# Two transformer blocks on one core: x and the meta tokens laid out turned by the host, small vectors in one block

## What is computed

```python
meta = broadcast(meta_tokens)                      # 16 tokens
x = concatenate([meta, x], axis=1)                 # 272 x 1024
h = rms_norm(x, attn_norm_g)                       # x * rsqrt(mean(x*x) + 1e-6) * g
proj = einsum('bld,de->ble', h, w_in)
qa, ka, va, qb, kb, vb = split(proj, splits)       # 512, 128, 128, 512, 512, 512 columns
qb = apply_rope(rms_norm(qb by heads of 64, b_q_norm_g), ang_b)      # the same for kb, qa, ka
lam = exp(sum(b_lambda_q1 * b_lambda_k1)) - exp(sum(b_lambda_q2 * b_lambda_k2)) + 0.2
```

## Time and profile before

| | |
|---|---|
| median of 3 runs | 814.72 us (813.7 to 815.52) |
| profiled execution, its own time | 815.82 us |
| its span, first to last instruction | 814.3 us |
| mean granted TensorE clock | 0.971 |
| busy: TensorE, VectorE, ScalarE, GpSimd | 96%, 57%, 46%, 14% |
| moved by DMA | 128.68 MB, 158 GB/s over the span |

### The profile page before, as it was taken

How to read it: one execution, slowest core, us unless ns; L and a number is a source line. 1 busy time by engine, 2 the same in 40 slices (tenths; PEclk the granted TensorE clock), 3 DMA queues, 4 the chain that set the end, 5 groups by cost and what they waited for, 6 DMA issues and landing times.

```text
span 814.3 us, 11050 instructions
## 1 busy us (share of the span) xinstructions
PE 779.4 (96%) x4468; PEld 676.4 (83%) x4468; DVE 465.1 (57%) x651; ACT 372.8 (46%) x539; POOL 110.4 (14%) x133
## 2 busy tenths in 40 slices
PE   5989897999999999999999999999988999999996
PEld 4777687789999999988888888887867998888995
DVE  3888734456555555555756666475586664444432
ACT  4454555245444444435543525383445554444431
POOL 3678305020000000003000000000020111111110
PEclk9999876999999999999999999999999999999999
DMA  9534204187666556633653545245372675555521
GB/s 222 181 97 132 79 1 130 36 271 227 215 190 188 183 171 193 182 101 119 204 195 114 198 150 192 70 131 198 136 232 81 217 245 184 184 183 185 188 64 52
DMA packets 70610, 128.68 MB, mean 158 GB/s; under 512 B 5264, under 2 KB 29056, under 8 KB 70560
## 3 DMA queue, kind: packets, MB, share of 16 engines
q1 hardware_dynamic: 68512, 123.75, 47.6%
q0 software_dynamic: 1808, 4.08, 2.1%
q10 hardware_dynamic: 240, 0.15, 0.1%
HBM read 126.85 MB, written 1.05 MB: 157 GB/s over the span
## 4 chain that ended last, share of the span: by engine, by line
PE 87%; DVE 5%; POOL 3%; ACT 2%; DMA 2%; issue 1%; SPq 0%; ACTq 0%; DVEq 0%; POOLq 0%
PE psum L372 45%; PE psum L653 27%; PE psum L419 3%; PE psum L515 2%; PE psum L583 2%; PE psum L672 2%; DMA w_raw<-in_w_in 2%; PE psum L773 1%; PE psum L434 1%; PE psum L559 1%; PE psum L713 1%; PE psum L443 1%; PE psum L397 1%; POOL head_square_sums L1662 1%; POOL vb_meta L1718 1%
## 5 line engine op out<-in xcount | busy, mean ns | idle before, releaser
L1156 DVE TENSOR_TENSOR w_lo<-w_raw,w_hi 128x1024 fp32r<-128x1024 f32 x224 | 272.2, 1239 | 159.9 <-ACT w_hi L820 158.8
L820 ACT ACTIVATE w_hi<-w_raw 128x1024 fp32r<-128x1024 f32 x232 | 238.1, 1061 | 154.7 <-PE psum L653 85.9
L653 PE MATMUL psum<-h_hi,w_hi 128*128 128x256 f32 x608 | 171.8, 283 | 1.3 <-DVE h_lo L1169 0.8
L653 PE MATMUL psum<-h_lo,w_hi 128*128 128x256 f32 x608 | 171.9, 283 | 0.0
L653 PE MATMUL psum<-h_hi,w_lo 128*128 128x256 f32 x608 | 171.2, 282 | 0.0
L372 PE MATMUL psum<-w_hi,h_hi 128*128 128x512 f32 (+1 forms) x352 | 141.7, 402 | 7.9 <-DVE w_lo L1156 4.6
L372 PE MATMUL psum<-w_hi,h_lo 128*128 128x512 f32 (+1 forms) x352 | 138.9, 395 | 0.0
L372 PE MATMUL psum<-w_lo,h_hi 128*128 128x512 f32 (+1 forms) x352 | 138.8, 394 | 0.0
L653 PEld LDWEIGHTS psum<-h_hi,w_hi 128*128 128x128 f32 x608 | 114.7, 189 | 2.6 <-issue 1.9
L653 PEld LDWEIGHTS psum<-h_hi,w_lo 128*128 128x128 f32 x608 | 114.9, 189 | 0.0
L653 PEld LDWEIGHTS psum<-h_lo,w_hi 128*128 128x128 f32 x608 | 114.3, 188 | 0.6
(11 more groups left out here) (301 smaller groups left out, 983.6 us busy)
## 6 DMA issues: line engine op xcount, KB each, us to landing
w_raw<-in_w_in SPq DMA_DIRECT2D x78, 512.0 KB, 4.6
w_raw<-in_w_down SPq DMA_DIRECT2D x54, 512.0 KB, 4.2
w_raw<-in_w_up SPq DMA_DIRECT2D x32, 512.0 KB, 4.6
w_raw<-in_w_gate SPq DMA_DIRECT2D x44, 256.0 KB, 2.9
w_raw<-in_w_up SPq DMA_DIRECT2D x44, 256.0 KB, 3.2
w_raw<-in_w_out SPq DMA_DIRECT2D x16, 512.0 KB, 4.4
w_raw<-in_w_branch_a SPq DMA_DIRECT2D x4, 512.0 KB, 5.1
w_raw<-in_w_branch_b SPq DMA_DIRECT2D x4, 512.0 KB, 5.2
```

The source lines that it names most:

```text
L653: mm = pe.matmul(outs, x[:, cols], y[:, kc, :], start=kc == 0 and n == 0, stop=kc == KC - 1 and n == 2)
L820: act.activation(T.w_hi[:, k % SLOTS, :], T.w_raw[:, k % RAW_SLOTS, :], ACT.Copy).then_inc(S.w_rounded, 1)
L1156: dve.tensor_tensor(T.w_lo[:, k % SLOTS, :], T.w_raw[:, k % RAW_SLOTS, :], T.w_hi[:, k % SLOTS, :], ALU.subtract).then_inc(S.w_cut, 1)
```

## The change

The host writes x and the meta tokens, transposed, into one array (turned, 128 x 8 x 272), the gains transposed, the rope table with the eight broadcast vectors as 4 KB rows for each partition (vectors, 0.5 MB), and ident with subln (small). On the chip:

- SyncE's queue has a quarter of turned ahead of each of the fills 0 to 3. Small, vectors and x itself come behind fill 5. GpSimd issues no early DMA.
- ScalarE's queue has gains, meta tokens and the meta rope rows.
- TensorE's transposes of gains, x and meta tokens are gone; its first instruction is the first product of slab "qb".
- ScalarE and VectorE take h_hi and h_lo straight from turned, which lies in the space of the later attention maps, chunk by chunk; fill 0 is rounded and cut in two halves, and the first product waits for the first half alone.
- The squares of x stand on ScalarE behind the rounding of fill 5, the mean on VectorE behind cut 5 and the lambda products; the meta tokens are scaled behind the last h_lo.

```diff
--- before.py
+++ after.py
...
+def laid_out(inputs):
+    arrays = {name: np.ascontiguousarray(inputs[name]) for name in _INS}
+    rope, arrays["rope2"] = rope_tables()
+    arrays["mask"] = masks()
+    tokens = np.concatenate([inputs["x"][0], inputs["meta_tokens"]], axis=0)
+    arrays["turned"] = np.ascontiguousarray(tokens.T.reshape(KC, P, KEYS).transpose(1, 0, 2))
+    gains = [inputs[name][0] for name in ("attn_norm_g", "ffn_norm_g", "norm_mix_pre_2", "norm_mlp_pre_2")]
+    arrays["gains"] = np.ascontiguousarray(np.stack(gains).reshape(4, KC, P).transpose(2, 0, 1))
+    arrays["small"] = np.ascontiguousarray(np.concatenate([np.eye(P, dtype=np.float32), inputs["b_subln_g"].T], axis=1))
+    rows = [rope[:SEQ].reshape(TILES, P, 4 * HD).transpose(1, 0, 2).reshape(P, TILES * 4 * HD)]
+    for name in ("a_q_norm_g", "a_k_norm_g", "b_q_norm_g", "b_k_norm_g", "b_lambda_q1", "b_lambda_k1", "b_lambda_q2",
+                 "b_lambda_k2"):
+        rows.append(np.broadcast_to(inputs[name], (P, HD)))
+    arrays["vectors"] = np.ascontiguousarray(np.concatenate(rows, axis=1))
+    arrays["rope1m"] = np.ascontiguousarray(rope[SEQ:])
+    return arrays
...
+    T.xt = T.maps[:, 0]
...
 def sync_program(nc, a, out, T, S, W):
     sp = nc.sync
-    for t in range(TILES):
-        sp.dma_start(T.x[:, t, :], a["x"][0, t * P:(t + 1) * P, :]).then_inc(S.x_landed[t], 16)
     for k, pieces in enumerate(W.fills):
         r = k % RAW_SLOTS
+        if k < KC // 2:
+            sp.dma_start(T.xt[:, 2 * k:2 * k + 2, :], a["turned"][:, 2 * k:2 * k + 2, :]).then_inc(S.turned_landed[k], 16)
+        if k == RAW_SLOTS + 2:
+            sp.dma_start(T.small[:], a["small"]).then_inc(S.small_landed, 16)
+            sp.dma_start(T.vectors[:], a["vectors"]).then_inc(S.small_landed, 16)
+            for t in range(TILES):
+                sp.dma_start(T.x[:, t, :], a["x"][0, t * P:(t + 1) * P, :]).then_inc(S.x_landed[t], 16)
...
@@ TensorE, slab @@
-            pe.wait_ge(*W.cut(S, k))
+            if not first or j > 0:
+                pe.wait_ge(*W.cut(S, k))
             for c in range(per):
                 kc = j * per + c
+                if first:
+                    pe.wait_ge(S.first_cut, kc + 1)
+                if first and j == 0:
+                    pe.wait_ge(*((S.half_cut, 1) if c == 0 else W.cut(S, k)))
...
-    pe.wait_ge(S.ident_landed, 16)
-    pe.wait_ge(S.gain_landed, 16)
-    pe.transpose(bank[7][:, 0:KC], T.gain_rows[0:KC, :], ident[0:KC, 0:KC]).then_inc(S.gains_turned, 1)
-    x_ready = [[(S.x_landed[t], 16)] for t in range(TILES)]
-    turn_pairs(T.x, (0,), (3,), x_ready)
-    turn_pairs(T.x, (1,), (4,), [(), ()])
-    turn_pairs(T.x, (2, 3), (5, 6), [(), ()])
-
-    def gains_and_meta():
...
-    slab("qb", KC, ((0,), (1,)), ready=CUT["h1"], between={(1, 1): gains_and_meta})
+    slab("qb", KC, ((0,), (1,)), first=True)
     slab("kb", KC, ((2,), (3,)), meta=4)
+    pe.wait_ge(S.small_landed, 32)
     pe.wait_ge(S.rope_done, ROTATED["qb"])
     turn_heads(T.qn, 4, (0, 1))
-    pe.wait_ge(S.gains_copied, 2)
     slab("kva", KC, ((5,), (6,)), meta=7)
...
@@ ScalarE @@
-    act.dma_start(T.ident[:], a["ident"]).then_inc(S.ident_landed, 16)
-    for n, name in enumerate(("attn_norm_g", "ffn_norm_g", "norm_mix_pre_2", "norm_mlp_pre_2")):
-        act.dma_start(T.gain_rows[n * KC:(n + 1) * KC, :], a[name][0].rearrange("(c p) -> c p", p=P)).then_inc(
-            S.gain_landed if n == 0 else S.gains_landed, 16)
+    act.dma_start(T.gains[:], a["gains"]).then_inc(S.gains_landed, 16)
     act.dma_start(T.xm[:], a["meta_tokens"]).then_inc(S.meta_landed, 16)
+    act.dma_start(T.rope1m[:], a["rope1m"]).then_inc(S.small_meta_landed, 16)
...
+    act.wait_ge(S.gains_landed, 16)
+    for j in range(KC // 2):
+        act.wait_ge(S.turned_landed[j], 16)
+        for c in range(2 * j, 2 * j + 2):
+            act.activation(T.h_hi[:, c, :], T.xt[:, c, 0:SEQ], ACT.Copy, scale=T.gains[:, 0, c:c + 1]).then_inc(
+                S.first_rounded, 1)
+        if j == 0:
+            act.wait_ge(S.w_landed[0], W.landed[0])
+            act.activation(T.w_hi[:, 0, 0:WIDE], T.w_raw[:, 0, 0:WIDE], ACT.Copy).then_inc(S.half_rounded, 1)
+            act.activation(T.w_hi[:, 0, WIDE:SLOT], T.w_raw[:, 0, WIDE:SLOT], ACT.Copy).then_inc(S.w_rounded, 1)
+            at.k = 1
+        elif j < KC // 2 - 1:
+            round_to(j + 1)
+    round_to(4)
+    act.wait_ge(S.meta_scaled, 1)
+    act.wait_ge(S.stack_set, 1)
+    act.activation(T.meta_stack[:, :, 0:META], T.meta_t[:], ACT.Copy).then_inc(S.meta_rounded, 1)
+    round_to(5)
     act.wait_ge(S.meta_landed, 16)
     act.activation(T.squares[0:META].rearrange("p a b -> p (a b)"), T.xm[:], ACT.Square,
                    accum_out=T.r_meta[:]).then_inc(S.meta_squared, 1)
-    round_to(4)
+    round_to(6)
+    square_rows(0, [[(S.x_landed[t], 16)] for t in range(TILES)])
     act.wait_ge(S.lam_summed, 1)
     act.activation(T.lam[:, 2:4], T.lam[:, 0:2], ACT.Exp).then_inc(S.lam_exped, 1)
...
     act.wait_ge(S.x_root, 1)
     act.wait_ge(S.meta_mean, 1)
     act.wait_ge(S.w_used, W.used("qb"))
...
@@ VectorE @@
+    dve.memset(T.zero[:].bitcast(F32), 0.0).then_inc(S.warm_set, 1)
     dve.memset(T.stat[:, 0:1], 0.0).then_inc(S.stat_set, 1)
...
+    dve.wait_ge(S.gains_landed, 16)
+    for j in range(KC // 2):
+        dve.wait_ge(S.turned_landed[j], 16)
+        for c in range(2 * j, 2 * j + 2):
+            dve.wait_ge(S.first_rounded, c + 1)
+            dve.scalar_tensor_tensor(T.h_lo[:, c, :], T.xt[:, c, 0:SEQ], T.gains[:, 0, c:c + 1], T.h_hi[:, c, :], ALU.mult,
+                                     ALU.subtract).then_inc(S.first_cut, 1)
+            if j == 0:
+                half = slice(c * WIDE, (c + 1) * WIDE)
+                dve.wait_ge(*((S.half_rounded, 1) if c == 0 else (S.w_rounded, 1)))
+                dve.tensor_tensor(T.w_lo[:, 0, half], T.w_raw[:, 0, half], T.w_hi[:, 0, half], ALU.subtract).then_inc(
+                    S.half_cut if c == 0 else S.w_cut, 1)
+        if j == 0:
+            at.k = 1
+        elif j < KC // 2 - 1:
+            cut_to(j + 1)
...
+    cut_to(6)
     lv = T.lamv[:].rearrange("p (j s) d -> p j s d", s=2)
-    dve.wait_ge(S.small_landed, 16 * SMALL_DMAS)
+    dve.wait_ge(S.small_landed, 32)
...
@@ GpSimd @@
-    small = [(T.rope1[:], a["rope1"][0:SEQ].rearrange("(t p) k d -> p t k d", p=P)), (T.rope1m[:], a["rope1"][SEQ:KEYS])]
-    small += [(T.hg[:, n, :], a[name][0:1, :].broadcast_to([P, HD]))
-              for n, name in enumerate(("a_q_norm_g", "a_k_norm_g", "b_q_norm_g", "b_k_norm_g"))]
-    small += [(T.lamv[:, n, :], a[name][0:1, :].broadcast_to([P, HD]))
-              for n, name in enumerate(("b_lambda_q1", "b_lambda_k1", "b_lambda_q2", "b_lambda_k2"))]
-    small += [(T.subln[:], a["b_subln_g"][0].rearrange("(p o) -> p o", o=1))]
-    assert len(small) == SMALL_DMAS
-    for dst, src in small:
-        pool.dma_start(dst, src, allow_slow_non_contiguous=True).then_inc(S.small_landed, 16)
...
     pool.wait_ge(S.half_set, 1)
-    pool.wait_ge(S.small_landed, 16 * SMALL_DMAS)
+    pool.wait_ge(S.small_landed, 32)
     rows_table("qb")
```

More of the change, by code:

```diff
@@ L45 @@
 SLOT = 1024
+SMALL = P + 1
+VECTORS = (TILES + 2) * 4 * HD
 def rope_tables():
@@ L192, in program @@
                        x_landed=[sems[f"x_landed{t}"] for t in range(TILES)],
+                       turned_landed=[sems[f"turned_landed{n}"] for n in range(KC // 2)],
                        post_landed=[sems[f"post_landed{t}"] for t in range(TILES)],
@@ L214, in allocate @@
     T.tmp = sb("tmp", [P, TILES, D])
-    T.ident = sb("ident", [P, P])
     T.gains = sb("gains", [P, 4, KC])
@@ L219, in allocate @@
     T.row_scale = sb("row_scale", [P, 4, TILES])
-    T.gain_rows = sb("gain_rows", [4 * KC, P])
+    T.small = sb("small", [P, SMALL])
+    T.ident = T.small[:, 0:P]
+    T.subln = T.small[:, P:P + 1]
     T.h_hi = sb("h_hi", [P, KC, SEQ], F32R)
@@ L225, in allocate @@
     T.xm = sb("xm", [META, D], c=one)
-    T.rope1 = sb("rope1", [P, TILES, 4, HD], c=one)
     T.rope1m = sb("rope1m", [META, 4, HD], c=one)
-    T.hg = sb("head_gains", [P, 4, HD], c=one)
-    T.lamv = sb("lam_vectors", [P, 4, HD], c=one)
-    T.subln = sb("subln", [P, 1], c=one)
+    T.vectors = sb("vectors", [P, VECTORS], c=one)
+    T.rope1 = T.vectors[:, 0:TILES * 4 * HD].rearrange("p (t k d) -> p t k d", t=TILES, k=4)
+    T.hg = T.vectors[:, TILES * 4 * HD:(TILES + 1) * 4 * HD].rearrange("p (n d) -> p n d", n=4)
+    T.lamv = T.vectors[:, (TILES + 1) * 4 * HD:VECTORS].rearrange("p (n d) -> p n d", n=4)
     T.meta_stack = sb("meta_stack", [P, KC, P], F32R, c=one)
@@ L374, in chunk, with slab @@
         return mm
-    def slab(name, chunks, outs, x_hi=T.h_hi, x_lo=T.h_lo, ready=None, meta=None, between=None):
+    def slab(name, chunks, outs, x_hi=T.h_hi, x_lo=T.h_lo, ready=None, meta=None, between=None,
+             first=False):
         per = W.per[name]
@@ L1235, in max1 @@
```

(20 more changed lines are left out.)

73 lines of the change are left out of this document (14 added, 59 removed).

## The result

| | before | after |
|---|---|---|
| median | 815.12 us (813.7 to 815.52, 4 runs) | 802.95 us (800.42 to 805.26, 4 runs) |
| profiled execution, span | 815.82, 814.3 | 800.42, 799.1 |
| mean granted TensorE clock | 0.971 | 0.985 |

The ratio is 0.9853, with the interval 0.9821 to 0.9885: 12.0 us faster (9.4 to 14.6), where 7.1 was forecast. One kernel of the experiments, before_shifted, took 1918 us in two of its ten executions, the traced one among them; they are left out of its ratio. The two profiled executions are 15.4 us apart, since each happened to lie on its own side of its median (short after, long before).

What follows compares the result with a forecast made beforehand. TensorE, busy 96% of the span, was taken as the bound, winnable where it waits or runs slowly. Turning at 6.7 + 26.2 + 2.3 = 35.2 instead of 42.35 gains 7.1 us: 807.6, range 803.0 to 812.0.

Steps and rivals of the forecast that it cites:

- Item 1: Start: with turned inputs the first product starts at 6.7 us (bounds 6.2 and 7.4), 4.9 earlier.
- Item 2: First fill: with no TensorE work ahead, the slab starts at low clock, losing 2.3 us (bounds 1.6 and 3.4).
- Item 3: Fill 0 in halves: spares the first product the other half's 1.2 us, already counted in the start.
- Item 4: Small vectors in one block: 365 GB/s between 9 and 18 us; fill waits of 1.2 and 1.7 us go.
- Item 5: x behind fill 5: x lands at 19.1 us, cut 6 at 26.7, wanted at 27.7; one microsecond to spare.
- Sum: Turning of the "qb" heads at 35.2 instead of 42.35, 7.1 us gained and carried to the end; 807.6.
- E: Rival: gain given back in GpSimd's stretch, its limit not being the turned heads; gain 0 to 2 us, 813.7; chance 0.07.
- B: Rival: late x makes TensorE wait for fill 6; at 290 GB/s gain 4.1 us, 810.6; chance 0.17.
- C: Rival: transfer rate does not recover; at 200 GB/s x lands at 32, 4.7 us slower, 819.4; chance 0.03.
- moves by the same 7.1: Behind the turning of the "qb" heads: everything to the end comes 7.1 us earlier, none added or lost.
- item 6: Rest: zero and ident moved, fewer semaphore waits; worth nothing, before the first fill or off the path.
- D: Rival, attention: shift changes low-clock stretches; 817 (chance 0.03) or gain 9 to 14 us, about 803 (chance 0.10).

Runs made afterwards that it cites:

- before_shifted: Kernel before with five more, already satisfied, waits for ident ahead of TensorE's first instruction; ratio 1.0004 (0.9993 to 1.0015).
- warm_wide: Kernel after with 12 useless products 512 wide, of ones, ahead of the first real product; 803.08 us, ratio 0.9856.
- rows_on_sync: Kernel after with the block of vectors replaced by the ten old small loads, issued by SyncE behind fill 5, ahead of x; 808.78 us, ratio 0.9932.
- before_again: Kernel before, unchanged, traced a second time; 813.53 us, ratio 0.9991.
- again: Kernel after, nothing edited, run once more; 802.24 us, ratio 0.9871.
- held: Kernel after with the first product also waiting for the cut of fill 3, giving back the start; 810.99 us, ratio 0.9965.
- padded: Kernel after with 508 unused bytes per partition ahead of the gains, restoring old addresses of tiles behind; 802.62 us, ratio 0.9858.
- pool_loads: Kernel after with the ten small loads back on GpSimd's queue at the start, in old form, ident staying on SyncE's; 808.85 us, ratio 0.994.

## Why the prediction was right, and where not

The side was right, and so was the mechanism of the start. By its own steps:

- **Item 1**, first product at 6.7: 6.97. The half fill was taken up at 5.47 (5.4), rounded in 0.63 and cut in 0.69. The gains were there at 3.91 and held nothing.
- **Item 2**, 2.3 us lost to a cold clock: 2.0 (ten steps 4.35, at full clock 2.34), and warm_wide shows that they are the clock's.
- **Item 3**, halves: worth 0.66 in the trace, about half of the 1.2 that they spare the first product, since the cold stretch ends at about the same time either way.
- **Item 4**, 365 GB/s between 9 and 18 us: 391. Both waits went, as the 60 products in one piece show. GpSimd's first table at 16.2: 17.09.
- **Item 5**, x at 19.1: 19.57. Squares of "qb" at 21.4: 21.74. Cut 6 at 26.7: 27.07; TensorE's first product of fill 6 starts at 27.65, so 0.6 us to spare where 1.0 was forecast. The 0.4 us from the last byte to the landing, which the sum for x uses, stands in no row. By the rates of the stretches (106 GB/s to 3 us, 356 to 9, 391 to 18) the 6.00 MB had moved by 18.1, 1.5 us before x was seen. The rate was better than forecast and this term worse, so that x came nearly on time is partly luck.
- **Sum**, turning at 35.2 instead of 42.35, 7.1 us: 7.25 between the chains. The start was 0.3 us later and the cold clock 0.3 us cheaper than forecast, which cancel. Behind it the lead is 7.22 at GpSimd's pieces: E is refuted.
- **B and C** did not come; rows_on_sync shows that B's mechanism is real, with x 4.3 us later (23.9 against 19.57) costing 5.3 us of the lead. B priced the wait at its length; the clock that falls in it was missing.

**The step that failed** is the sentence that everything behind the turning "moves by the same 7.1", together with item 6, "nothing". In the eleven rows of the table that have the change, gain less lead lies between 1.8 and 5.6 us, 3.8 on average, at leads from -0.7 to 8.3; in before_again it is 0.5. So a microsecond of the start is worth one, and 3.8 us more come with the change whatever the start does. Of them:

- 2.8 us (12.13 at 344, 14.96 near the end) come behind 344 us. 0.8 of it is a low stretch of 3.4 us at 621 or 623 us, in both traces of before and in none of after, again, held and padded. 1.6 are the pace of products 512 wide, 11.24 and 11.15 us for 48. The other 0.4 are three pieces of 96 products 256 wide near the end, 11.39 us where before has 11.52. No rival had this. It is not the start (held has it), not the addresses (padded), not a chance of one trace (again, before_again), and not the count of waits ahead (before_shifted, by its time). What it is stays open.
- 1 us is left over, and where it comes from is not shown. In the first pair of traces 1.7 + 2.7 us come in attention, as rival D's good side has it, and before_again takes back 2.0 of them. With low stretches of equal length none is left (padded against before_again). The mean granted clock is 0.981 in ten executions of the kernel after, 0.982 in eight of held and 0.977 in 17 of before beside them. That doesn't show shorter stretches in attention either: both traces of before have two low stretches of 3.4 us outside attention that after lacks (at 53 or 61 us and at 621 or 623), and by my estimate these two alone lower the mean by 0.004 (half of 6.8 us in 813). And held has the higher clock without being earlier, so a shift by 7 us is not what brings it.

D had been given 0.10 with a gain of 9 to 14 us. The size came true, but at most a quarter of the excess can be D's. That the median came so near to the range is owed to the room left for D, and that is luck.

## What to carry to other kernels

A stretch in which all DMA engines are busy and move less than half of what they do elsewhere is worth looking into by queue and by packet before anything is reordered: here eight rows of 256 bytes read for all partitions, and one load by single elements, cost the start up to 8 us, and the same data laid out by the host as 4 KB rows cost 0.6 us of it early on GpSimd's queue and none that shows behind fill 5 on SyncE's. Ahead of a cold start, judge an earlier first instruction by what it brings later on: the products that come first are slow ones, so 1.15 us earlier was worth 0.66. And when a sum made at one place in the chain is carried to the end, say which later stages have a clock or a pace of their own; two traces of the unchanged kernel would have shown 2 us of play there.

## What the runs showed of the hardware

- Products 512 wide at full clock, back to back, took 11.24 us for 48 in one program and 11.15 in another with the same products. Between 412 and 529 us the same values come back in both traces of each program, to 0.02 us. Behind 650 us the two are closer: 11.14 to 11.25 by turns in before, 11.13 to 11.21 in after. Most pieces of 96 products 256 wide took 11.51 or 11.52 us in both; the kernel after has four of 11.39, the kernel before none.
- With the same ten small loads under way, the 16 DMA engines were 0.98 busy at 275 GB/s, fills among them, when GpSimd had issued the loads (pool_loads, 9 to 18 us), and 0.21 busy at 50 GB/s when SyncE had (rows_on_sync, 15 to 20 us).
- A wait of 3.9 us in rows_on_sync was followed by seven steps of 0.4 to 0.6 us where 0.23 is usual (granted clock 0.51 from 31.2 to 34.6 us), so it cost 1.6 us beyond its length.
- 44 products of zeros 128 wide, back to back for 9.65 us, left the next seven steps at 0.44 us; 12 products of ones 512 wide in 5.3 us left them at 0.23. Width and data differ at once here, so which of them matters isn't told apart.
- The low clock in attention came in stretches of 6.8, 10.2, 13.6 or 17.1 us, differently in executions of one and the same program, and spans followed: 799.1 us at a mean clock of 0.986, 806.3 at 0.973.
